# Three tiles begun at stage entries, pool sums in two memories, an earlier turn of the ada rows, and another table of moved mixer steps

## The reference, cut to what matters

```python
def first_block(...):
    for layer in range(2):
        g = norm_gain[layer]
        f = swiglu(rms_norm(h, g[0]), w_gate[layer, 0], w_up[layer, 0], w_down[layer, 0])
        h = h + 0.5 * rms_norm(f, g[1])
        hm = rms_norm(h, g[2])
        mix = pool_mixer(hm, ...) if layer == 0 else dilated_mixer(hm, ...)
        h = h + rms_norm(mix, g[3])
        f = swiglu(rms_norm(h, g[4]), w_gate[layer, 1], w_up[layer, 1], w_down[layer, 1])
        h = h + 0.5 * rms_norm(f, g[5])

def pool_mixer(h, w_in, w_group, scale, w_out):
    u = h @ w_in
    # channel group g has window w = 2, 4, 8, 16: p = (sum of the last w rows of u) / count - u
    y = einsum('bsgc,gcd->bsgd', p, w_group) * scale
    return y @ w_out

def mixer_layer(x, cx, c, c_ctx, ...):            # twice, in the second block
    shift, scale, gate = split(silu(c) @ w_ada + b_ada, 3)
    h = x * (1 + scale) + shift                   # the context likewise
    ... = split(h @ w_in)                         # gated scan, attention, differential, window
    y = concat(four mixers) * silu(g_lat)
    return layer_norm(alpha * x + gate * (y @ w_out))
```

## Time and profile before

| what | value |
|---|---|
| median of three executions | 3254.57 us |
| the three | 3253.49, 3254.57, 3260.31 us |
| the profiled execution | 3257.69 us |
| its span in the trace | 3255.9 us |
| TensorE busy | 3101.4 us, 95% |
| VectorE, ScalarE, GpSimd busy | 1439.4, 1152.0, 1453.4 us |
| mean granted TensorE clock | 0.98 of full |

### The profile page before, as it was taken

The page is one execution under the profiler, slowest core; times in us unless marked ns, Lnnn a source line. Parts: engine busy times, 40 slices in busy tenths (PEclk is TensorE's granted clock), DMA queues, the critical chain, the costliest instruction groups (busy, mean ns, idle before and its releaser), DMA issues.

```text
span 3255.9 us, 55259 instructions
## 1 busy us (share of the span) xinstructions
PE 3101.4 (95%) x20586; PEld 2370.9 (73%) x20586; DVE 1439.4 (44%) x2931; ACT 1152.0 (35%) x1975; POOL 1453.4 (45%) x2267
## 2 busy tenths in 40 slices
PE   8999989999999999999999999988999998899998
PEld 6888767888778886777778877766666676666665
DVE  3232464222532225344442224575466435675654
ACT  3222333222332224111232224454444525554554
POOL 4555675555655556333355544442244132343423
PEclk9999999999999999999999999998999999999999
DMA  4222423322342223211143242200010111111011
GB/s 150 97 97 97 142 82 135 97 97 97 124 140 96 97 96 132 66 59 59 53 137 98 101 136 91 85 28 21 27 40 22 72 53 65 40 34 46 32 55 59
DMA packets 74358, 264.75 MB, mean 81 GB/s; under 512 B 7856, under 2 KB 9136, under 8 KB 73904
## 3 DMA queue, kind: packets, MB, share of 16 engines
q1 hardware_dynamic: 69584, 246.02, 22.8%
q10 hardware_dynamic: 4576, 15.98, 1.3%
HBM read 252.53 MB, written 7.34 MB: 80 GB/s over the span
## 4 chain that ended last, share of the span: by engine, by line
PE 84%; DVE 10%; ACT 4%; issue 2%; DMA 0%; DVEq 0%; POOL 0%; SPq 0%; ACTq 0%
PE ps L1674 29%; PE ps L1703 19%; PE ps L1679 14%; PE ps L2231 3%; PE ps L2204 2%; PE ps L2254 2%; PE ps L1667 2%; PE ps L2098 1%; DVE ps L2405 1%; DVE xl L2397 1%; PE ps L2037 1%; DVE hc L2412 1%; PE ps L2284 1%; DVE tb L2563 1%; DVE tb L2932 1%
## 5 line engine op out<-in xcount | busy, mean ns | idle before, releaser
L1155 POOL TENSOR_TENSOR wl<-raw,wh 128x256 fp32r<-128x256 f32 x1640 | 1212.4, 772 | 1488.3 <-ACT wh L1270 862.6
L1292 ACT ACTIVATE wh<-raw 128x1024 fp32r<-128x1024 f32 x224 | 237.9, 1062 | 945.3 <-PE ps L1679 857.5
L1674 PE MATMUL ps<-xh,wh 128*128 128x512 f32 x1392 | 543.6, 390 | 2.4 <-ACT pr L1370 2.0
L1674 PE MATMUL ps<-xl,wh 128*128 128x512 f32 x1392 | 541.6, 389 | 0.0
L1270 ACT ACTIVATE wh<-raw 128x1024 fp32r<-128x1024 f32 x186 | 196.8, 1058 | 437.2 <-PE ps L1703 267.5
L1679 PE MATMUL ps<-xh,wl 128*128 128x512 f32 x1392 | 344.4, 389 | 2.7 <-POOL wl L1155 2.7
L1674 PEld LDWEIGHTS ps<-xh,wh 128*128 128x128 f32 x1392 | 261.3, 188 | 59.0 <-issue 3.8
L1679 PEld LDWEIGHTS ps<-xh,wl 128*128 128x128 f32 x1392 | 261.0, 188 | 58.4 <-POOL wl L1155 4.3
L1674 PEld LDWEIGHTS ps<-xl,wh 128*128 128x128 f32 x1392 | 261.3, 188 | 54.9 <-issue 1.0
L1674 PE MATMUL ps<-ah,wh 128*128 128x512 f32 x748 | 292.2, 391 | 0.8 <-DVE al L2550 0.8
L1674 PE MATMUL ps<-al,wh 128*128 128x512 f32 x748 | 291.1, 389 | 0.0
(11 more groups left out here) (371 smaller groups left out, 4856.2 us busy)
## 6 DMA issues: line engine op xcount, KB each, us to landing
raw<-wts_dram SPq DMA_DIRECT2D x458, 512.0 KB, 3.5
spilled_dram<-hc ACTq DMA_DIRECT2D x1, 3072.0 KB, 10.7
hc<-spilled_dram ACTq DMA_DIRECT2D x1, 3072.0 KB, 10.2
tb<-tab_dram ACTq DMA_DIRECT2D x5, 512.0 KB, 3.7
spilled_dram<-hc ACTq DMA_DIRECT2D x1, 2048.0 KB, 7.2
hc<-spilled_dram ACTq DMA_DIRECT2D x1, 2048.0 KB, 8.4
out_dram<-hc SPq DMA_DIRECT2D x8, 256.0 KB, 2.1
hc<-x_dram SPq DMA_DIRECT2D x7, 256.0 KB, 6.7
```

Of the source, the lines that this page charges most:

```text
L1155: ins = pool.tensor_tensor(wl[:, n % SPLIT, piece], raw[:, LOADED[n] % RAW, piece], wh[:, n % SPLIT, piece].bitcast(F32), ALU.subtract)
L1292: act.activation(wh[:, n % SPLIT, :], raw[:, at % RAW, :], ACT.Copy).then_inc(hi_done, 1)
L1674: pe.matmul(out_, wh[:, s, k * P:(k + 1) * P], x_(k, at), start=first, stop=False)
```

## The change

1. **Three tiles at four entries.** The pool and the ffn 0,1, ffn 1,0 and ffn 1,1 stages begin three tiles rather than two (`enter`). The extra tile's `wh` and `wl` live in columns 512 to 639 of `xh` and `xl`, which are free in these stages; in the pool stage the ring of weight tiles is three long by this all through. Each entry issues the two products with `xh` as soon as ACT has rounded the chunk (`part_hi`), and only the product with `xl` waits for `x_ready`. The third tile runs five chunks behind and its last three chunks come after the sum of squares. The dilated entry uses the same code with two tiles, and `first_two_tiles` (first stage, and both mixer entries) also starts its first tile's products on `part_hi`. The ada tiles of a three tile entry are loaded after the third tile.
2. **Pool sums in SBUF and PSUM.** For the six tiles of windows 16, 8 and 4, each padded sum is written twice, once in SBUF and once in PSUM banks 4 to 7, and each add reads one of each. That is 18 added DVE instructions of 128x512 and one memset. `POOL_READY[2]` goes from 4 to 6; a group tile issues its products with `wh` first and all with `wl` last.
3. **The rows turned earlier.** At the end of ffn 1,1 `turn_ada` comes before the down tile m = 6 instead of after the sum of squares, DVE finishes the conditioning terms before it waits for the inverse root, and ACT starts each chunk of mixer layer 0's input with the context part, which needs no residual.
4. **Angles.** One of seven angle steps of DVE moves from down tile 6 to tile 1 of ffn 0,1.
5. **The table.** About 80 entries of `MOVED` differ.

The core of the diff:

```diff
-POOL_READY = {2: 4, 3: 2, 1: 6, 0: 8}
+LAST_IN = (0, 1)
+ANGLE_PARTS = ((0,), (1, 2), (3,), (4,), (5,), (6,))
+POOL_READY = {2: 6, 3: 2, 1: 6, 0: 8}
+TURN_AT = 6
...
+RINGS_OF_3 = ("pool", )
+AHEAD = tuple(n for (name, k), at in zip(STAGE_TILES, STAGE_AT)
+              for n in (range(at, at + k, 3) if name in RINGS_OF_3 else (at,) if at in ENTRIES else ()))
+THIRD_LAG = 5
...
-        ((("step", 1, 5), ("quarter", ("q", 3), 1), ("update", 1, 5), ("rms", 0), ("quarter", ("q", 3), 2)), ("turn", 0)),
+        ((("step", 1, 5), ("weights", 1, 4), ("update", 1, 5), ("rms", 0), ("quarter", ("q", 3), 2)), ("turn", 0)),
...
+        ((("quarter", ("v", 2), 3),), ("rows", 2)),
...
+        def weights_of(w, n, k, count=1):
+            if n in AHEAD:
+                return (xh if w is wh else xl)[:, k:k + count, SEQ:SEQ + P]
+            return w[:, slot_of(n), k * P:(k + count) * P].rearrange("p (k c) -> p k c", c=P)
...
+            def enter(banks_):
+                n0, x0, h0_ = c.take("tile", len(banks_)), c.take("x", KC), c.take("part hi", KC)
...
+                pe.wait_ge(lo_done, n0 + 1)
+                for k in range(ADA_FIRST):
+                    ada_beside(n0, k)
+                for k in range(KC):
+                    pe.wait_ge(part_hi, h0_ + k + 1)
+                    high_low_weights(n0, banks_[0], k)
+                    if k == 0:
+                        pe.wait_ge(lo_done, n0 + 2)
+                    high_low_weights(n0 + 1, banks_[1], k)
+                    if len(banks_) == 2 and k + ADA_FIRST < KC:
                         ada_beside(n0, k + ADA_FIRST)
+                    if len(banks_) == 3 and k >= ADA_FIRST:
+                        ada_beside(n0, k)
+                    if len(banks_) == 3 and k >= THIRD_LAG:
+                        third(k - THIRD_LAG)
+                    pe.wait_ge(x_ready, x0 + k + 1)
+                    for j in range(2):
+                        ins = low_chunk(n0 + j, banks_[j], k)
+                        if k == KC - 1:
+                            ins.then_inc(tile_done, 1)
+                sum_squares()
+                if len(banks_) == 3:
+                    for k in range(KC - THIRD_LAG, KC):
+                        ins = third(k)
+                    ins.then_inc(tile_done, 1)
...
                 for m in range(KC):
+                    if ("ffn", layer, i) == ADA_LOOP and m == TURN_AT:
+                        turn_ada()
...
+                    if in_bank:
+                        dve.tensor_tensor(bank_pads[:, 0, PAD:], ps[:, n % 4, :], rs, ALU.mult)
                     took(dve.tensor_tensor(pads[:, 0, PAD:], ps[:, n % 4, :], rs, ALU.mult), n)
...
+                        if in_bank:
+                            if 2 * step < w:
+                                dve.tensor_tensor(pads[:, dst, PAD:], bank_pads[:, src, PAD:], shifted, ALU.add)
+                            own(dve.tensor_tensor(bank_pads[:, dst, PAD:], bank_pads[:, src, PAD:], shifted, ALU.add))
```

More of the change, by code:

```diff
@@ L177, in enter @@
     def enter(*stage):
-        if len(plan) - entered[0] == 2 and stage in ADA_STAGES:
+        if len(plan) - entered[0] == (2 if stage == ("dilated",) else 3) and stage in ADA_STAGES:
             ada(2)
@@ L423 @@
         ((("weights", 0, 0),), ("quarter", ("g", "s0"), 0)),
-        ((("values", 0, 0),), ("operands", 0, 4)),
-        ((("weights", 0, 2),), ("decay", 0, 5)),
+        ((("values", 0, 0),), ("quarter", ("g", "s0"), 2)),
+        ((("operands", 0, 4),), ("update", 0, 3)),
+        ((("products", 0, 4), ("take", 0, 4)), ("weights", 0, 2)),
         ((("sums", 1, "abs"),), ("products", 0, 5)),
@@ L436 @@
         ((("update", 1, 1),), ("shift", 1)),
-        ((("values", 0, 7), ("end", 0), ("operands", 1, 3)), ("math", 1)),
+        ((("end", 0), ("operands", 1, 3)), ("step", 1, 2)),
         ((("quarter", ("k", 2), 2),), ("dist", 1, 5)),
+        ((("math", 1),), ("products", 1, 3)),
         ((("weights", 1, 0),), ("weights", 1, 1)),
@@ L463 @@
         ((("rope", ("k", 4)),), ("decay", 3, 1)),
-        ((("dist", 3, 3), ("keep", 2)), ("rows", 3)),
-        ((("operands", 3, 1),), ("weights", 3, 0)),
+        ((("quarter", ("v", 3), 3), ("keep", 2)), ("step", 3, 0)),
+        ((("dist", 3, 3), ("rows", 3)), ("operands", 3, 1)),
         ((("products", 3, 1),), ("weights", 3, 1)),
@@ L497 @@
         ((("dist", 4, 3),), ("exps", 0, 5)),
-        ((("dist", 4, 4), ("weights", 0, 0)), ("quarter", ("g", 0), 2)),
+        ((("rows", 0), ("quarter", ("g", 0), 2)), ("products", 4, 2)),
+        ((("dist", 4, 4),), ("weights", 0, 0)),
         ((("decay", 4, 3), ("take", 4, 2)), ("values", 0, 0)),
@@ L1219, in _ @@
                 elif name in ("ffn", "pool", "dilated"):
-                    remainders(used)
+                    remainders(used - 2)
+                    for n in range(used - 2, used + (used - 2 in AHEAD)):
+                        remainder(n)
+                        c.take("tile")
                     c.take("part", KC)
@@ L1813, in wait_x, with first_two_tiles @@
                 pe.wait_ge(x_ready, c.at("x"))
-            def first_two_tiles(tiles, with_squares=False, lag=0, summed=False, ada=False):
-                n0, x0 = c.take("tile", 2), c.take("x", KC)
+            def first_two_tiles(tiles, with_squares=False, lag=0):
+                n0, x0, h0_ = c.take("tile", 2), c.take("x", KC), c.take("part hi", KC)
                 pe.wait_ge(lo_done, n0 + 1)
@@ L1877, in ffn @@
                 f_norm()
-                if (layer, i) != (0, 0):
+                if (layer, i) != (0, 0) and ("ffn", layer, i) != ADA_LOOP:
                     turn_ada()
@@ L1884, in pool @@
                 a0, x0 = c.take("a", KC), c.take("x", KC)
-                for what, g0 in POOL_TILES[2:]:
+                c.take("part hi", 2 * KC)
+                for what, g0 in POOL_TILES[3:]:
                     n = high_tile()
```

222 lines of the change are left out of this document (154 added, 68 removed).

## The result

The changed kernel takes 3228.62 us in the median of five executions (3220.45 to 3233.81) against 3254.57: 25.95 us less, a ratio of 0.9911 with a 95% interval of 0.9896 to 0.9926. The profiled execution took 3227.86 us.

The account below looks back on a forecast made before the run. TensorE, busy 95% of the span, was taken as the bound, with 154 us of idle time and low-clock products to win. Stage edits -13.3 and table -8 made -21.3 us, median 3233 us, range 3220 to 3246.

Parts of the forecast that it names:

- Entries of the ffn stages: Entries of ffn 0,1, ffn 1,0 and ffn 1,1: chunks 5 to 7 keep TensorE without pause, 1.8 us each, -5.4 us.
- Dilated: Dilated stage's entry: two products instead of nine follow the last remainder, -1.7 us.
- Pool: Pool stage: VectorE's adds at 0.69 us give -3.9; later sum, memset and extra products cost; sum -2.2 us.
- the rival with slow adds: Pool: VectorE is held with one SBUF operand as well, six tiles take 69 us instead of 40; 3266 us, chance 0.04.
- Ada phase: Layer 0's ada phase: 4.6 us leave the chain, the turn between down tiles costs 3.7, smaller savings 0.6 and 0.7; -2.2 us.
- Starts: First stage and mixer layer 1's entry: two products of a chunk go ahead of the remainder's wait, -0.8 us each.
- The table: Mixers: moved steps fill TensorE's waits, some at the low clock; -8 us, bounds +3 and -20.
- The two moves that were priced: First mixer layer, at `weights` (1, 4) and `rows` (2): independent work fills two waits of over 2 us; 6.2 us.
- the table gives twice as much: Rival, mixers: the clock is held through more of them; 3224 us, chance 0.08.
- The table gives nothing: Rival, mixers: a wait filled on TensorE can come back at the next unit; 3241 us, chance 0.22.
- The low clock at the ffn entries: Rival, stage entries: issuing on `part_hi` makes more short pauses and the clock falls, +6 us; 3239 us, chance 0.09.
- The third tile was there in time: Rival, entries: the third tile comes late and TensorE waits at chunk 5; entries gain nothing, 3240 us, chance 0.08.

Follow-up runs that it names:

- the run that took it away: The changed kernel with all pool sums in SBUF again, nothing else undone: 3230.54 us, ratio 0.9932; pool stage 129.0 us against 124.7.
- the run of the two moves: Kernel before with only weights (1, 4) behind step (1, 5) and the last quarter of v 2 ahead of rows (2): 3251.61 us, ratio 0.9982.
- the split by layer: Kernel before with the change's table for the second mixer layer alone: 3244.85 us, ratio 0.9957.

## Why the prediction was right, and where it was not

The time was right by luck: two sizes were off in opposite directions. The edits in the stages gave 4.8 us or less where 13.3 were forecast, and the table about 24 to 26 where 8 were.

- **Entries of the ffn stages, "-5.4 us" and "-0.2" for the angle step: about 2.1 was there.** ffn 0,1 gained 0.4 and ffn 1,0 0.8; ffn 1,1 0.9, as the run with the turn late shows (379.4 against 380.4). The working of the entry was right in its mechanism, and 0.85 us short in its sizes (8.5 us for the chunks 5 to 7 where 8.2 were forecast, 3.85 for the last 15 products where 3.4 were). The step that failed is "What is late next is the sum of squares ... so I cost that at nothing": at the end of ffn 0,1 it is VectorE that is late, and half of the 0.95 us was lost there. The entry's gain was also put down to the wrong part. The run with two tiles shows that the third tile gave nothing and that the early starts on the rounded part are what shortened the entry; the third tile moved products ahead of the sum of squares, but TensorE has them to do either way.
- **Dilated, "-1.7": 1.0 at the entry, on average nothing at the end.** Counted from the sum ahead of it, the entry fell from 23.55 to 22.52; the wait of 0.34 us for GpSimd's square was not in the forecast. The stage as a whole took 369.5 to 370.6 us in ten profiles of the changed entry and 370.0 to 370.1 in four of the old one, so the gain is lost behind the entry; why was not tried.
- **Pool, "-2.2": 1.8 and 1.5.** The term of VectorE, -3.9, measured as 4.1 in the tiles and 4.35 by the run that took it away. The later sum was 1.1 us, not 0.6. In the rival with slow adds "12 for the rest" doesn't fit the 1.2 us a tile of the sum, which make 7.2 for six tiles; the rival did not come, so nothing hangs on it.
- **Ada phase, "-2.2": a loss of 0.8.** The 4.6 us and the 1.3 of the two smaller terms were there together (the phase is 6.0 us shorter, and VectorE's 3 us of idle time are gone). But ffn 1,1 is 5.9 us longer although its entry gained 0.9, so the turn cost 6.8, not 3.7. The step that failed is "I take 3.7, since TensorE is dense there": it was dense and the clock fell all the same, in the turn itself, and the down tile behind it paid. In four lots, at full clock, the turn cost 3.8 and the term came to -2.1, close to the forecast.
- **Starts, "-0.8" each:** ffn 0,0 1.1 to 1.3, though that stage differs by up to 3 us between profiles of the same code (382.3 to 385.4); layer 1's entry with the output 0.2 to 0.4.
- **The table, "-8 us": 22 to 29 in the profiles, 26 by the ratio of the run of the table alone.** The two moves that were priced fit, 6.2 forecast, 2 to 9 measured. The step that failed is "All the other seventy moves ...; -0.8 for them". Of 14.4 us of idle time that went, the run of the two moves shows 2.2 as theirs, no more than the old table's own scatter. What went lay mostly in short waits of both layers: TensorE's waits between 1 and 2 us summed to 35.9 us in 25 places before and to 22.6 in 16 after, those of 2 us and more to 14.0 before and 10.4 after. Beside that the same products took less busy time, 8.4 us in the mean of the profiles, some of it in stretches where nothing was forecast to change (2284 to 2668). Which single moves gave it was not tried beyond these two and the split by layer.
- **The rivals:** "the table gives twice as much", with the clock held through more of the mixers, is the one that came true for its part, at three times the forecast's 8 us, while its time of 3224 was no nearer than the forecast's. The table gives nothing: out, by the run of the table alone. The low clock at the ffn entries did not come in sum: 0.86 against 0.93 before at ffn 1,0, but 1.00 against 0.93 at ffn 1,1. The third tile was there in time; at ffn 1,0 it was an ada tile, loaded behind it, that came late. Of the last one, VectorE held with one SBUF operand, the 0.69 us of the adds says no, and GpSimd's 0.783 says that the holding was mutual, as the Trainium skill, page "SBUF — State Buffer", section "Who interferes with whom", has it.

## What to carry to other kernels

Price a long list of small reorderings by the sum of the waits that it touches, in every layer that it touches, and allow for the clock: here half as much again as the idle time came back as shorter busy time. Read the clock by stretch in both profiles before calling a gain idle time, and in several profiles before calling it a gain. For an edit that starts work earlier at a stage's entry, look at what is last at that stage's end. Where very small products must go between long ones, try them in short lots: here that gave 3.0 us against one block.
